# Token tiles staggered at stage ends, outputs by halves, own buffers for the last down piece, the gate through DRAM, four adaptive-norm chunks first

## The chip, the cores and the metric

One core of a Trainium2 chip. The time is the device time of one execution in microseconds; of a kernel before, the median of its runs is given. The kernel's two token tiles have 128 tokens each, all arithmetic is on 32-bit data.

## The reference, cut to what matters

Two blocks of two layers each run one after the other on x (256 tokens, 1024 channels). A layer has three stages, each of this form:

```
mod   = silu(c) @ ada_w[l] + ada_b[l]            # 9 x 1024 values: shift, scale, gate for 3 stages
n     = rmsnorm(x, g[j]) * (1 + scale[j]) + shift[j]
x     = x + factor * gate[j] * stage(n)          # first block: 1 + gate; factor 0.5 for an ffn, 1 for a mixer
ffn   : (silu(n @ w_gate) * (n @ w_up)) @ w_out  # 2816 hidden channels
mixer : layer 0 gated linear recurrence (hgrn2), 1 differential attention,
        2 and 3 sparse attention plus a gated mlp; each ends in an output projection 1024 x 1024
```

After layer 3 a last rmsnorm with its own gain. A stage is called (l,j) here, l from 0 to 3, j = 0 and 2 for an ffn, 1 for a mixer.

## The kernel before, in words

**Products.** TensorE multiplies each 32-bit product as three products of reduced-precision float parts: high by high, high by low, low by high (times_three, L1367). So each piece of weights (128 x 2048 values, 1 MB, two DMAs) that lands in `raw` (ring of 3) is cut: ScalarE writes its high part to `wH` (cut, L456), VectorE subtracts it for the low part `wL` (cut, L782). A piece may be loaded once the low part of the piece 3 before is done (s_split), and its high part is written once TensorE has used the piece 3 before (s_eaten). Everything that loads is issued by SyncE, in one order written out by hand.

**Ffn.** The hidden channels go in 11 groups of 256. A group has two up pieces (channels 0 to 3 and 4 to 7 of the input) and one down piece: 33 pieces, numbered 0 to 32. Group c's up products go into PSUM `GU` (bank i for token tile i), ScalarE takes silu of the gate half (L515), VectorE multiplies (L883) into `sh`, TensorE transposes it into `TM` (L1421), ScalarE writes the high part `hH` (L524), VectorE the low part `hL` (L887), and TensorE adds the down products into `PY` (two banks per token tile). TensorE's order in turn c: up piece 0, transposes of group c-1, up piece 1, down of group c-1, with both token tiles in each. At the end stand transposes and the down piece of the last group alone.

**Boundary** (boundary, L847, on VectorE; norm, L477, on ScalarE; norm_and_first, L1393, on TensorE). x tile i gets the gated output of `PY` (L841 scale over 1024 columns, L845 add); ScalarE squares it and takes the root; VectorE makes a diagonal matrix of 1/rms (L861); TensorE multiplies x by it, which transposes and scales (turn_x, L1385, L1389); VectorE (channels 0 to 3, L868) and ScalarE (4 to 7, L495) apply scale and shift; ScalarE and VectorE write high and low parts `xH` (L490) and `xL` (L874), two channels at a time; TensorE starts the first two pieces of the stage, tile 0 channels 0 to 5, turn_x of tile 1, then the rest. The pieces that are cut meanwhile: the next stage's piece 0 before the last hidden high part in ScalarE's queue, piece 1 ahead of the outputs, piece 2 at the end.

**Gate.** The gate is a column per 128 channels in `mod`. VectorE spreads it (L833), TensorE multiplies by the identity (gate_broadcast, L1378), ScalarE copies it to `gB`, where each partition has all 1024 values (L511).

**Adaptive norm.** The 18 chunks of 512 values of mod per layer are computed by VectorE, four products over 1024 values a chunk (L793), from 2 MB each. 8 chunks of layer 0 are done at the start through a ring of 5 in `M`, the other chunks one per group in the loops of the ffns: 10 in (l,0), 8 of the next layer in (l,2). Small constants of the mixers are loaded in (0,0) (late_constants, L379).

**Mixers** end in four projection pieces (project, L1494), each over both token tiles.

Of the kernel before, what the change touches and what calls it, by code (L numbers as in the profile page):

```python
# [116 lines left out]
def build(nc, T, out, upto=99):  # L117

    with ExitStack() as ctx:
# [20 lines left out]
        xL = sb("xL", [P, ND, S], F32R)  # L140
        hH = sb("hH", [P, 2, S], F32R)
# [11 lines left out]
        vb = sb("vb", [P, 5 * P])  # L153
# [12 lines left out]
        acc = sb("acc", [P, 4])  # L166
        modf = M[:, 0:2 * D].rearrange("p (t d s) -> p t d s", t=NT, d=ND)
# [50 lines left out]
        sg_ = [ada[:, n, :].rearrange("p (t n) -> p t n", t=NT) for n in range(2)]  # L218
        pec = sb("pec", [P, 2])
# [32 lines left out]
        s_x = sem("s_x")  # L252
        s_ss = sem("s_ss")
# [11 lines left out]
        s_gp = sem("s_gp")  # L265
# [50 lines left out]
        ADA_FIRST, ADA_REST = 8, 10  # L316
# [6 lines left out]
        def ada_turns(l, j):  # L323

            if j == 0:
                return l, ADA_FIRST, ADA_REST
            return (l + 1, 0, ADA_FIRST) if l + 1 < 4 else (l, 0, 0)

# [5 lines left out]
        def _(sp):  # L334
# [18 lines left out]
            def load_mixer(w, pieces):  # L353

                at = 0
                for k0, lo, width in pieces:
                    load(w[:, at:at + 4 * width], 4 * width)
                    at += 4 * width

            def load_start(c, q):  # L360
# [5 lines left out]
                sp.dma_start(start_[slot], T["ada_t"][0, 2 * c + q]).then_inc(s_start[slot], 16)  # L366
# [5 lines left out]
            def load_ada(l, c, q):  # L372
                v = T["ada_t"][l].rearrange("(c q) p n -> q p c n", q=2)
# [5 lines left out]
            def late_constants():  # L379
# [3 lines left out]
                for at, n, name in ((0, P, "a_onorm"), (P, P, "b_qk_g"), (2 * P, P, "b_subln"),  # L383
                                    (3 * P, 2 * P, "b_lam")):
                    sp.dma_start(vb[:, at:at + n], T[name].rearrange(
# [3 lines left out]
            def ffn(l, j):  # L389
                load_up(l, j, 0, 0)  # L390
                load_up(l, j, 0, 1)
                if (l, j) == (0, 0):
                    late_constants()
                if (l, j) == (1, 2):
                    sp.wait_ge(s_adafree, ADA_RING + 2 * (2 * ADA_REST + ADA_FIRST))
                    load_cond(1)
                la, c0, turns = ada_turns(l, j)

                def loop(first, count, with_ada):
                    with sp.Fori(0, count) as i:  # L400
# [4 lines left out]
                        if with_ada:  # L405
                            load_ada(la, c0 + i, 0)
                        load_up(l, j, first + i, 1)
                        if with_ada:
                            load_ada(la, c0 + i, 1)
# [1462 lines left out]
```

## Time and profile before

| | |
|---|---|
| median of 3 runs | 2488.42 us (2483.75 to 2490.06) |
| profiled execution | 2491.22 us, its span 2489.6 us |
| TensorE busy | 2273.3 us, 91% |
| VectorE busy | 1654.5 us, 66% |
| ScalarE busy | 1097.5 us, 44% |
| HBM read | 529.19 MB, 213 GB/s over the span |
| chain that ended last | TensorE 81%, VectorE 9%, ScalarE 5% |

Times are from the span's start. Busy time is a sum over the whole span; what a change at a boundary does is read from the timeline there. On TensorE's rows, the idle time in brackets counts from the end of the instruction before, which is modelled and overlaps the next one, so a product of 512 columns shows 0.39 us and follows the one before after 0.23. SPq rows are the issue of DMAs by SyncE, with the waits between merged issues inside. The ends of the 8 ffns are at about 259, 675, 871, 1226, 1423, 1854, 2050 and 2478, those of the 4 mixers at 477, 1027, 1657 and 2280.

### The profile page before, as it was taken

To read this page: it belongs to the slowest core of one execution; us is meant where nothing else is said; L and a number is where in the kernel's file an instruction comes from. 1 tells how busy PE (TensorE), PEld (TensorE's weight loads), DVE (VectorE), ACT (ScalarE), POOL (GpSimd) and SP (SyncE) were. 2 spreads that over 40 slices of the span, in tenths; PEclk is the share of its full clock that TensorE was granted. 3 is DMA by queue.
4 is the path that set the end of the run, shared out by engine and by line. 5 is a ranking of instruction groups with operands and counts; after the bars stand their busy time and mean duration, and the time that the engine had idled before them with its cause. 6 is when DMAs were issued, how large, how long until landed. Compare 5 with 4: busy or idle time off the path is not lost.

```text
span 2489.6 us, 30572 instructions
## 1 busy us (share of the span) xinstructions
PE 2273.3 (91%) x11004; PEld 1900.7 (76%) x11004; DVE 1654.5 (66%) x2245; ACT 1097.5 (44%) x1225; POOL 0.2 (0%) x4
## 2 busy tenths in 40 slices
PE   0999995899999997899999998999999999899998
PEld 0788884688788875788788787778878888777886
DVE  7677576677577776587577754468767776446444
ACT  1444543343444355434443444544344445464433
POOL 0000000000000000000000000000000000000000
PEclk9999997899999997999999997899999999799999
DMA  9687430388578731387588732348857883223553
GB/s 382 265 319 279 161 136 0 136 310 311 204 265 312 273 143 70 129 335 281 193 311 308 284 128 85 102 162 316 298 203 274 320 310 128 85 102 126 179 202 110
DMA packets 126426, 531.30 MB, mean 213 GB/s; under 512 B 14736, under 2 KB 15504, under 8 KB 107280
## 3 DMA queue, kind: packets, MB, share of 16 engines
q1 hardware_dynamic: 126352, 530.30, 58.8%
q8 instruction: 48, 0.79, 0.1%
q14 instruction: 26, 0.21, 0.0%
HBM read 529.19 MB, written 1.05 MB: 213 GB/s over the span
## 4 chain that ended last, share of the span: by engine, by line
PE 81%; DVE 9%; ACT 5%; issue 2%; DMA 2%; SPq 1%; DVEq 0%; ACTq 0%
PE GU L1371 14%; PE GU L1375 14%; PE GU L1373 14%; PE PY L1371 9%; PE PY L1373 9%; PE PY L1375 9%; DVE wL L786 2%; ACT wH L461 2%; PE PY L1389 2%; PE TM L1421 1%; DMA M<-in_ada_t 1%; PE GU L1758 1%; PE PY L1668 1%; DVE M L793 1%; DVE x L845 1%
## 5 line engine op out<-in xcount | busy, mean ns | idle before, releaser
L786 DVE TENSOR_TENSOR wL<-raw,wH 128x2048 fp32r<-128x2048 f32 x352 | 794.6, 2279 | 280.9 <-ACT wH L461 279.3
L461 ACT ACTIVATE wH<-raw 128x2048 fp32r<-128x2048 f32 x352 | 659.6, 1899 | 203.4 <-PE PY L1375 102.4
L1371 PE MATMUL GU<-wH,xH 128*128 128x512 f32 (+1 forms) x1600 | 635.2, 397 | 31.6 <-DVE xL L874 13.2
L1375 PE MATMUL GU<-wH,xL 128*128 128x512 f32 (+1 forms) x1600 | 623.8, 390 | 0.0
L1373 PE MATMUL GU<-wL,xH 128*128 128x512 f32 (+1 forms) x1600 | 623.3, 390 | 0.0
L1371 PEld LDWEIGHTS GU<-wH,xH 128*128 128x128 f32 x1600 | 302.8, 189 | 97.1 <-issue 32.6
L524 ACT ACTIVATE hH<-TM 128x512 fp32r<-128x512 f32 x88 | 52.7, 598 | 691.5 <-PE TM L1421 691.5
L1375 PEld LDWEIGHTS GU<-wH,xL 128*128 128x128 f32 x1600 | 302.3, 189 | 63.7
L1373 PEld LDWEIGHTS GU<-wL,xH 128*128 128x128 f32 x1600 | 303.0, 189 | 58.5
L793 DVE CUSTOM_DVE_ANT_0 ada<-ada,cond 128x1024 f32<-128x1024 f32 x256 | 298.0, 1220 | 0.0
L887 DVE TENSOR_TENSOR hL<-TM,hH 128x512 fp32r<-128x512 f32 x88 | 60.9, 691 | 253.8 <-ACT hH L524 253.7
L1371 PE MATMUL PY<-wH,hH 128*128 128x512 f32 x704 | 218.0, 391 | 12.5 <-DVE hL L887 12.4
L1373 PE MATMUL PY<-wL,hH 128*128 128x512 f32 x704 | 217.6, 390 | 0.0
L1375 PE MATMUL PY<-wH,hL 128*128 128x512 f32 x704 | 217.3, 390 | 0.0
L1371 PE MATMUL PY<-wH,xH 128*128 128x512 f32 x432 | 177.2, 410 | 8.2 <-DVE wL L786 6.8
L1373 PE MATMUL PY<-wL,xH 128*128 128x512 f32 x432 | 173.6, 402 | 0.0
L1375 PE MATMUL PY<-wH,xL 128*128 128x512 f32 x432 | 172.5, 399 | 0.0
L1371 PEld LDWEIGHTS PY<-wH,hH 128*128 128x128 f32 x704 | 131.7, 188 | 41.5 <-issue 10.3
L1375 PEld LDWEIGHTS PY<-wH,hL 128*128 128x128 f32 x704 | 132.7, 188 | 27.8
L1373 PEld LDWEIGHTS PY<-wL,hH 128*128 128x128 f32 x704 | 132.5, 188 | 27.7
L1371 PEld LDWEIGHTS PY<-wH,xH 128*128 128x128 f32 x432 | 84.8, 196 | 27.0 <-issue 5.5
L515 ACT ACTIVATE sh<-GU 128x512 f32<-128x512 f32 x88 | 52.7, 599 | 118.3 <-PE GU L1375 118.3
(275 smaller groups left out, 2013.9 us busy)
## 6 DMA issues: line engine op xcount, KB each, us to landing
raw<-in_up_w SPq DMA_DIRECT2D x352, 512.0 KB, 6.2
ada<-in_ada_t SPq DMA_DIRECT2D x128, 1024.0 KB, 8.1
raw<-in_down_w SPq DMA_DIRECT2D x176, 512.0 KB, 4.8
raw<-in_c_w SPq DMA_DIRECT2D x96, 512.0 KB, 4.3
raw<-in_a_w SPq DMA_DIRECT2D x40, 512.0 KB, 4.2
M<-in_ada_t SPq DMA_DIRECT2D x16, 1024.0 KB, 10.5
raw<-in_b_w SPq DMA_DIRECT2D x32, 512.0 KB, 4.3
M<-in_cmp_w SPq DMA_DIRECT2D x4, 1024.0 KB, 9.2
```

Of the source, the lines that this page charges most:

```text
L461: act.activation(wH[:, slot, 0:words], raw[:, slot, 0:words], ACT.Copy).then_inc(s_high, 1)
L515: act.activation(sh[:, 0, :, :], GU[:, :, 0:CF], ACT.Silu).then_inc(s_silu, 1)
L524: act.activation(hH[:, :, :].rearrange("p f s -> p (f s)"), TM[:, 0, :], ACT.Copy).then_inc(s_hh, 1)
L786: dve.tensor_tensor(wL[:, slot, 0:words], raw[:, slot, 0:words], wH[:, slot, 0:words], ALU.subtract).then_inc(s_split, 1)
L793: ins = dve.tensor_tensor_reduce(w, w, cond[:, :], 1.0, 0.0, ALU.mult, ALU.add, acc[:, 2 * q + b:2 * q + b + 1])
L845: dve.tensor_tensor(x[:, i, :], x[:, i, :], xn[:, i, :], ALU.add).then_inc(s_x, 1)
L887: dve.tensor_tensor(hL[:, :, :].rearrange("p f s -> p (f s)"), TM[:, 0, :], hH[:, :, :].rearrange("p f s -> p (f s)"), ALU.subtract).then_ ...
L1371: pe.matmul(outs[i], aH, wh[i], start=first, stop=False)
L1373: pe.matmul(outs[i], aH, wl[i], start=False, stop=False)
L1375: ins = pe.matmul(outs[i], aL, wh[i], start=False, stop=last)
L1389: ins = pe.matmul(PT[:, i, d, :], x[:, i, d * P:(d + 1) * P], diag[:, i, :], start=True, stop=True)
L1421: ins = pe.transpose(TM[:, 0, f * S + i * P:f * S + (i + 1) * P], sh[:, 1, i, f * P:(f + 1) * P], ident)
```

## The change

Start: 4 chunks instead of 8 at the start, x loaded after the fourth half; squares and roots of x between them. The chunks of the first block's layer 0 that follow: 10 in (0,0), one inside hgrn's second half after `q_` is gated, one after its last two low parts, 10 in (0,2). late_constants is issued after the last chunk's loop in (0,0).

Stage ends: in the last group of an ffn each step is done by token tile. The last down piece has its own `lastH`, `lastL`, tile 1's hidden parts their own `hHt`, `hLt`. Outputs are scaled and added by halves of 512 columns. The next stage's cuts may start a piece earlier. Mixers' last two pieces run tile 0 of both, then tile 1 of both. The last norm and the output DMA go by tile.

Gate: gcol is written to a DRAM tensor (`gates`, one row per stage, 1024 elements, not contiguous on the side of the core) and read back broadcast over 128 partitions, both by SyncE. The spread, the 8 products and the copy are gone.

The diff, cut; engine names are put ahead of hunks:

```diff
# SyncE
+            def gate_out():
+                n = t.next("gate")
+                sp.wait_ge(s_gcol, n)
+                sp.dma_start(T["gates"][n - 1].rearrange("(d p) -> p d", p=P), gcol[:, :],
+                             allow_slow_non_contiguous=True).then_inc(s_gd, 16)
+            def gate_in():
+                n = t.next("gate", 0)
+                sp.wait_ge(s_gd, 16 * n)
+                if n > 1:
+                    sp.wait_ge(s_x, NT * (n - 1))
+                sp.dma_start(gB[:, :], T["gates"][n - 1:n].broadcast_to([P, D])).then_inc(s_gb, 16)
-            def load_mixer(w, pieces):
+            def load_mixer(w, pieces, l):
...
+                    if l == 0 and n == 16:
+                        load_ada(MIXER_CHUNKS[0], 0)
+                        load_ada(MIXER_CHUNKS[0], 1)
+                    if n == 6:
+                        gate_out()
+                    if n == 10:
+                        gate_in()
...
                 if turns:
                     loop(1, turns, 1)
+                if (l, j) == (0, 0):
+                    late_constants()
                 if turns < NF - 1:
                     loop(1 + turns, NF - 1 - turns, 0)
+                gate_out()
                 load_down(l, j, NF - 1)
+                gate_in()
# ScalarE
+            def cut(words=PIECE, early=0):
+                slot, to = t.next("piece") % RING, t.next("weights") % RING
+                act.wait_ge(s_raw[slot], t.next(s_raw[slot], 32))
+                act.wait_ge(s_eaten, t.next(s_eaten) - early)
+                act.activation(wH[:, to, 0:words], raw[:, slot, 0:words], ACT.Copy).then_inc(s_high, 1)
+            def squares(i, first=False):
...
-                    root(i, (l, j) == PHASES[0])
-                    if i == 0:
-                        cut()
+                    if before:
+                        squares(i)
+                        root(i)
+                    if before and i == 0:
+                        cut(early=before == "ffn")
...
-                act.wait_ge(s_gp, t.next(s_gp))
-                act.activation(gB[:, :], TMf, ACT.Copy).then_inc(s_gb, 1)
+                cut(early=before == "ffn")
...
+                loop(NF - 2)
+                cut()
+                cut()
+                cut_last()
+                hidden_high()
                 if (l, j) != PHASES[-1]:
-                    cut()
-                hidden_high()
-                t.next("done")
+                    cut(early=1)
+                silu_tile(0)
+                high_tile(0)
+                silu_tile(1)
+                root_table()
+                high_tile(1)
# VectorE
+            def outputs_0(before):
+                dve.wait_ge(s_gb, t.next(s_gb, 16))
+                for h in range(2):
+                    dve.wait_ge(s_y, t.next(s_y))
+                    output(0, h)
+                if before == "ffn":
+                    low_tile(1)
...
                 columns(l, j)
-                cut()
-                if pieces:
-                    dve.wait_ge(s_gb, t.next(s_gb))
-                    dve.wait_ge(s_y, t.next(s_y))
-                    gated_output(0)
-                    add_output(0)
+                if before:
+                    outputs_0(before)
+                    root(0)
+                    scaled_identity(0)
+                    outputs_1(before, pieces)
...
-                        if pieces and i == 0 and b == 1:
-                            add_output(1)
+                        if before and i == 0 and b == 1:
+                            cut()
                 cut()
...
+                cut()
+                if turns == NF - 1:
+                    chunk(c0)
+                cut()
+                hidden_low()
+                cut_last()
+                hidden_tile(0)
                 if (l, j) != PHASES[-1]:
                     cut()
-                hidden_low()
+                low_tile(0)
+                hidden_tile(1)
# VectorE, hgrn
+                    if grp == 1:
+                        chunk(MIXER_CHUNKS[0])
...
                 cut()
                 cut()
+                chunk(MIXER_CHUNKS[1])
# TensorE
-                gate_broadcast()
                 turn_x(0)
                 slots = [t.next("piece") % RING for _ in range(2)]
-                pe.wait_ge(s_split, t.next(s_split, 2))
...
+                        if i == 0 and d % 4 == 0:
+                            pe.wait_ge(s_split, t.next(s_split))
...
+                        if by_tile and i == 0 and d == ND - 1:
+                            ins.then_inc(s_up, 1)
...
-                turn(True)
-                loop(NF - 2)
-                pe.wait_ge(s_h, t.next(s_h))
-                turn_hidden()
-                down(False, True)
+                pe.wait_ge(s_h, t.next(s_h))
+                token_tile(GU[:, 0, :], 0, slot, 0)
+                pe.wait_ge(s_h, t.next(s_h))
+                token_tile(GU[:, 1, :], 0, slot, 1).then_inc(s_eaten, 1)
...
+                loop(NF - 3)
+                pe.wait_ge(s_h, t.next(s_h))
+                up(0)
+                turn_hidden()
...
+                token_tile(GU[:, 0, :], 1, ups, 0).then_inc(s_up, 1)
...
+                down_tile(0, downs, False)
+                pe.wait_ge(s_h, t.next(s_h))
+                turn_tile(0)
+                token_tile(GU[:, 1, :], 1, ups, 1).then_inc(s_eaten, 1)
...
+                down_last(0)
+                pe.wait_ge(s_h, t.next(s_h))
+                turn_tile(1)
+                down_tile(1, downs, False).then_inc(s_eaten, 1)
+                pe.wait_ge(s_hl, t.next(s_hl))
+                down_last(1)
...
+            def project_last(q):
+                slots = [t.next("piece") % RING for _ in range(2)]
+                for i in range(NT):
+                    for h in range(2):
+                        if i == 0:
+                            pe.wait_ge(s_split, t.next(s_split))
+                        token_tile(PY[:, 2 * i + 1, :] if q is None else PY[:, 2 * i + h, :], h if q is None else q,
+                                   slots[h], i).then_inc(s_eaten if i else s_y, 1)
```

## Rows read from the trace of the kernel before

**Rows 1.** The page, part 1: busy time, share and instructions of each engine.
```profile
PE 2273.3 (91%) x11004; PEld 1900.7 (76%) x11004; DVE 1654.5 (66%) x2245; ACT 1097.5 (44%) x1225; POOL 0.2 (0%) x4
```

**Rows 2.** Waits of TensorE over the span: total us, times, longest.
```profile
PE PY L1371 <- DVE hL L887: 12.4, 8, 1.9
...
PE GU L1371 <- issue: 11.6, 8, 1.5
PE PY L1389 <- DVE M L861: 10.8, 12, 2.1
```

**Rows 3.** Timeline of the start: start us, us, instruction, idle before and releaser.
```profile
9.11 1.22 DVE L793 CUSTOM_DVE_ANT_0 M<-M,cond 128x1024 f32<-128x1024 f32 x1 [8.24 <-DMA M<-in_ada_t]
...
10.00:15.00 5.00, 0.00 (x0) 0.00 (x0) 4.93 (x10) 0.00 (x0) 0.00 (x0) 1.00 1.01 424
...
51.58 1.91 ACT L461 ACTIVATE wH<-raw 128x2048 fp32r<-128x2048 f32 x1 [44.88 <-DMA raw<-in_up_w]
...
67.09 0.77 PE L1371 MATMUL GU<-wH,xH 128*128 128x512 f32 x1 [3.92 <-DVE xL L874]
```

**Rows 4.** Timeline of the boundary from (0,2) to (1,0).
```profile
669.74 0.70 PE L1371 MATMUL PY<-wH,hH 128*128 128x512 f32 x2 [1.50 <-DVE hL L887]
...
672.98 1.22 DVE L841 TENSOR_TENSOR xn<-PY,gB 128x1024 f32<-128x1024 f32 x1
...
675.30 1.95 PE L1381 MATMUL TM<-cst,sh 128*128 128x128 f32 x16
...
677.70 2.05 PE L1389 MATMUL PY<-M,x 128*128 128x128 f32 x16 [0.45 <-DVE M L861]
...
680.81 0.47 PE L1371 MATMUL GU<-wH,xH 128*128 128x512 f32 x1 [1.06 <-DVE xL L874]
...
681.52 1.22 DVE L845 TENSOR_TENSOR x<-x,xn 128x1024 f32<-128x1024 f32 x1
...
695.26 0.47 PE L1371 MATMUL GU<-wH,xH 128*128 128x512 f32 x1 [1.46 <-issue]
```

**Rows 5.** Timeline of two boundaries after mixers, (0,1) and (1,1).
```profile
462.23 6.70 DVE L786 TENSOR_TENSOR wL<-raw,wH 128x2048 fp32r<-128x2048 f32 x3 [0.57 <-ACT wH L461]
...
484.46 0.77 PE L1371 MATMUL GU<-wH,xH 128*128 128x512 f32 x1 [0.24 <-DVE xL L874]
...
1027.08 1.95 PE L1381 MATMUL TM<-cst,sh 128*128 128x128 f32 x16
...
1031.12 3.46 PE L1389 MATMUL PY<-M,x 128*128 128x128 f32 x16 [2.10 <-DVE M L861]
...
1034.83 0.52 PE L1371 MATMUL GU<-wH,xH 128*128 128x512 f32 x1 [0.25 <-DVE xL L874]
```

**Rows 6.** Timelines of the start, (2,0) and (3,0); then issues by tile, KB, us to landing.
```profile
41.45 0.43 SPq L380 DMA_DIRECT2D cst<-in_table  x1
...
47.46 1.04 SPq L385 DMA_DIRECT2D vb<-in_b_lam  x1
...
1411.60 1.92 ACT L461 ACTIVATE wH<-raw 128x2048 fp32r<-128x2048 f32 x1 [2.11 <-DMA raw<-in_c_w]
...
2020.11 2.86 SPq L343 DMA_DIRECT2D raw<-in_down_w  x4
...
2031.38 0.60 PE L1421 MATMUL TM<-cst,sh 128*128 128x128 f32 x4
...
2039.66 1.92 ACT L461 ACTIVATE wH<-raw 128x2048 fp32r<-128x2048 f32 x1 [1.57 <-DMA raw<-in_c_w]
...
vec<-in_vec_cols SPq DMA_DIRECT2D x1, 240.0 KB, 4.4
...
posi<-in_positions SPq DMA_DIRECT2D x1, 1.0 KB, 14.8
```

**Rows 7.** Timeline of the end: first and last instruction of VectorE after the last product.
```profile
2478.92 1.23 DVE L841 TENSOR_TENSOR xn<-PY,gB 128x1024 f32<-128x1024 f32 x1 [0.17 <-PE PY L1375]
...
2483.75 1.29 DVE L1359 SCALAR_TENSOR_TENSOR x<-x,rstd,M 128x1024 f32<-128x1024 f32 x1
```

More of the change, by code:

```diff
@@ L576, in hgrn @@
             def hgrn():
-                norm(0, 1)
+                norm(0, 1, "ffn")
                 cut()
@@ L676, in nsa @@
             def nsa(l):
-                norm(l, 1)
+                norm(l, 1, "ffn")
                 cut()
@@ L767, in _ @@
                     nsa(l)
+                before = "mixer" if j == 1 else "ffn"
             if len(PHASES) == 12:
                 for i in range(NT):
+                    squares(i)
                     root(i)
@@ L847, in boundary, with chunk, output @@
-            def boundary(l, j, pieces):
+                    dve.tensor_scalar(gcol[:, :], gate, factor, None, ALU.mult).then_inc(s_gcol, 1)
+            def chunk(c):
+                ada_products(0)
+                ada_products(1)
+                ada_store(c, s_adafree, t.next(s_adafree, 2))
+            def output(i, h):
+                half = slice(h * 512, (h + 1) * 512)
+                chained(dve.tensor_tensor(xn[:, i, half], PY[:, 2 * i + h, :], gB[:, half], ALU.mult))
+                dve.tensor_tensor(x[:, i, half], x[:, i, half], xn[:, i, half], ALU.add
+                                  ).then_inc(s_x if h else s_xs, 1)
@@ new lines, in outputs_0, with outputs_1 @@
+            def outputs_0(before):
[5 more added lines that the diff above has]
+                    low_tile(1)
+            def outputs_1(before, pieces):
+                if before == "ffn":
+                    dve.wait_ge(s_y, t.next(s_y))
+                    t.next("done", pieces - 1)
+                else:
+                    dve.wait_ge(s_eaten, t.next("done", pieces - 1))
+                output(1, 0)
+                dve.wait_ge(s_eaten, t.next("done"))
+                output(1, 1)
@@ L1330, in _ @@
                 start_products(1)
-                ada_store(0, c, s_startfree, 2 * c + 2)
-            pieces = 0
-            for n, (l, j) in enumerate(PHASES):
-                if n == 0 or PHASES[n - 1][1] == 1:
-                    cut()
-                boundary(l, j, pieces)
+                ada_store(c, s_startfree, 2 * c + 2)
+                if c > 1:
+                    root(c - 2)
+                    scaled_identity(c - 2)
+            before, pieces = None, 0
+            for l, j in PHASES:
+                if before is None:
+                    cut()
+                if before != "ffn":
+                    cut()
+                boundary(l, j, before, pieces)
+                if j == 1:
+                    gate_column(l, j)
                 if j != 1:
@@ L1344, in _ @@
                     nsa(l)
+                before = "mixer" if j == 1 else "ffn"
                 pieces = 3 * NF if j != 1 else PIECES[l] - (22 if l > 1 else 0)
-            dve.wait_ge(s_gb, t.next(s_gb))
-            dve.wait_ge(s_y, t.next(s_y))
-            gated_output(0)
-            add_output(0)
-            dve.wait_ge(s_eaten, t.next("done", pieces))
-            gated_output(1)
-            add_output(1)
+            outputs_0(before)
             if len(PHASES) == 12:
@@ L1423, in turn_hidden, with down_tile, down @@
                 ins.then_inc(s_ht, 1)
-            def down(first, last):
+            def down_tile(i, slot, first):
+                for f in range(2):
+                    a = slice(i * P, (i + 1) * P)
+                    halves = [slice(f * D + h * 512, f * D + (h + 1) * 512) for h in range(2)]
+                    ins = times_three([PY[:, 2 * i + h, :] for h in range(2)], hH[:, f, a], hL[:, f, a],
+                                      [wH[:, slot, b] for b in halves], [wL[:, slot, b] for b in halves],
+                                      first and f == 0, False)
+                return ins
+            def down(first):
                 slot = t.next("piece") % RING
```

338 lines of the change are left out of this document (201 added, 137 removed).

## The prediction, made before the result was known

> **What bounds the kernel now.** The page comes first: TensorE is busy for 2273.3 of 2489.6 us [rows 1], so only the 216 us in which it isn't busy, and work that can be made shorter, are to be had. The waits of TensorE, summed, come next [rows 2]: apart from the wait at the very start they are small and regular. It waits 12.4 us (8 times 1.5) for the low part of the last hidden piece, 11.6 us (8 times 1.46) as "issue" after the first up pieces, 10.8 us for the diagonal of the norm. Each lies at a stage boundary. The timeline of the first stage [rows 3], of a boundary after an ffn [rows 4] and after a mixer [rows 5] shows what happens there, and SyncE's timeline with ScalarE's waits [rows 6] what the transfers do. Last the end of the kernel [rows 7].
>
> The profiled execution took 2491.2 us (span 2489.6, 1.6 around it), 2.8 above the median of 2488.4. I make the sum against 2491.2 and take 2.8 off.
>
> **Start (four chunks first).** The first x product starts at 67.09 [rows 3]. The first piece of weights arrived at 51.58 because 17 MB stood ahead of it. Four chunks mean 4.2 MB less. At 9.11 about 1.9 MB have landed (first product [rows 3]); 7 chunk halves, x and piece 0 (9.4 MB) follow at 424 GB/s [rows 3]: 22.3 us, so piece 0 is there at 31.4. VectorE is no faster: half a chunk needs two products of 1.22 [rows 3], and each of the last four halves waits for its MB, so the eighth ends at about 31, and with both roots behind it at 33. ScalarE's cut of piece 0 stands behind the second root in its queue: to 34.8. The low parts, 2 x 2.2 us, end at 39.4; the scale columns and the step to the first product (677.70 to 680.81 less 1.2 for the transposes, which have long been done [rows 4]: 1.9) give 41.4. Gain 25.7, bounds 20 (everything serial behind the second piece) and 29 (bytes alone). The 4 chunks moved cost VectorE 4.9 us each: two in a loop turn of (0,2), where it has 3 us to spare in 16.8, one in hgrn's tail under the output projection, and chunk 15 before the boundary, below.
>
> **End of an ffn.** With the tiles staggered, other products (a piece of 24 takes 5.56 us, 669.74 to 675.30 [rows 4], so 12 products 2.7) stand between each transpose and the product that needs its low part. The 1.5 us before the last down piece [rows 4] goes at all 8 ends: 12.4 [rows 2]. Then tile 0's output: before, its scaling began 2.3 us before the end of the last down piece, and from there to the diagonal took 4.7 (672.98 to 677.70 [rows 4]). Now tile 0 is complete 5.4 us before the end (down_last(0), then turn, down_tile(1), down_last(1)), halves overlap, so the diagonal is ready about 2 us early. The 2.4 us from 675.30, in which the broadcast of 1.95 hides, to 677.70 goes. Tile 1's last half (2 x 0.62) is ahead of VectorE's first modulation and gives back 0.2. So 2.2 x 7 = 15.
>
> **End of a mixer.** The stretch from the last projection to the first up product is 7.75 us at 1027.08 [rows 5], 6.9 and 7.7 at two like it. Left is the 3.1 us that turn_x(0) takes to the product plus 0.3: gain 4.3, 3.5, 4.3, and 0.9 at two of them for products at the lower clock (the transposes take 3.46 instead of 2.05 [rows 4, 5]): 13. In hgrn VectorE stands in the way: three low parts (462.23, 6.70 us [rows 5]), now with chunk 15 (4.9) among them, so it is free for output 0 only at 474.3, the diagonal comes at 478.6, and both halves of tile 1 run to 481. First up product 483.0 instead of 484.46 [rows 5]: gain 1.5. Together 14.7.
>
> **New waits inside the boundary.** Piece 1 of a stage is now cut on VectorE between the low parts of channels 3 and 4. Before, an add of 1.22 us stood there (681.52 [rows 4]) and hurt nobody. A cut of 2.29 ends at 683.84, the low part 0.43 later; TensorE has used up channels 0 to 3 at 683.6. Loss 0.75 at 11 boundaries: 8.2. After the first up pieces 1.46 was lost 8 times [rows 2, 4]. Tile by tile, silu of tile 0 could start 5 us earlier, but ScalarE now has cut (1.9) and table load (1.28) ahead of it and VectorE a cut; I work out 0.7 left, nothing in (0,0). Gain 0.76 x 7 + 1.2 = 6.5. Net of both -1.7.
>
> **The gate through DRAM.** Removed: on VectorE the spread, on TensorE the broadcast, on ScalarE the copy, all of them already hidden. Added: per stage one write of 1024 single elements, a wait for it on SyncE, one broadcast read of 512 KB. SyncE has every load behind that wait. The trace has no such write. The nearest from below is the vector load of 240 KB, 4.4 us to landing; from above the positions, 256 single elements, 14.8 us, but behind a table of 1.3 MB [rows 6]. I take 7, nearer to the lower, since the queue is nearly empty there; both ends stay in the range's cases. In a mixer four pieces lie between write and read and cover it. At an ffn's end the write goes out behind the load of piece 31 (the down piece before the last), the read and everything of the next stage behind it. Look at (3,0): piece 31 is issued at 2020.11 [rows 6], the write 2021.0, landed 2028. Then come the read and, ahead of the next piece, the mixer's own 3.2 MB: with piece 33 that is 4.8 MB, 11.4 us, so it lands at 2041 (before: cut at 2039.66, with ScalarE already waiting for it [rows 6]). Before, only the last hidden piece stood behind that cut. Now it stands ahead of the silu of tile 0, whose product TensorE needs two half pieces after the transposes of 2031.38 [rows 6], plus 5.4 and 0.44: at 2037.3. Cut 1.9 and silu and product 0.9: 2043.8. Stall 6.5. At (2,0) landing was already 1411.60 [rows 6]; by the same steps 6.6. At (0,0) the late constants are new before the write: 41.45 to 48.5, 7.05 us of issue [rows 6], 1.6 MB. Piece 32 and with it the low part stall 3, piece 33 another 3: 6. At (1,0), (0,2), (1,2), (2,2) piece 33 lands 1 to 4 us before it is needed: 0. After two of the stalls the clock will fall, as behind the gap of 4 us in [rows 5]: 1.4 (3.46 for 2.05), 1.5 each with what follows. Loss 6.5 + 6.6 + 6 + 3 = 22.
>
> The Trainium skill speaks against this edit too ("DMA: Bandwidth & Descriptors", Rules for kernel authors): a last dimension that isn't contiguous becomes one descriptor per element. Its "Anatomy of one DMA" puts a fixed cost of about 2 us on each DMA, most of it the receipt, heaviest toward HBM; neither is shown by a row here. With 2 us in the place of 7, an estimate by that page, the three stalls would be 15 us smaller; with many descriptors the rule points the other way.
>
> **End of the kernel.** From the last product (2478.75) to the last scaling (2483.75 + 1.29 [rows 7]) was 6.3 us, with a scale and an add of 1.23 each over 1024 columns and a square of 1.06. With halves, and tile 0 long done, 4.6; the last DMA is half as long. Gain 2.
>
> **Sum.** 25.7 + 12.4 + 15 + 14.7 - 1.7 - 22 + 2 = 46. 2491.2 - 46 - 2.8 = 2442.
>
> **Rivals.**
> A, the stalls don't come: the write lands in 3 us or less and the piece behind it is in time. For it: before, ScalarE waited only 1.6 us for this piece at (3,0) [rows 6]. Against: bandwidth alone, without any round trip, puts it at 2039.7, too late for 2037.3. With 5 of the 22 left: 2442 - 17 = 2425.
> B, the write takes 12 us: 5 more at the three stalled ends, 4 at two, 1 at two more: 25, so 2467.
> C, slower than before: the same place, SyncE waiting for the write with the next stage's loads behind it. With a us more than 7 the loss is 3a + 2(a - 1) + 2(a - 4); it eats the 46 at a = 8, so from a write of 15 us. At 20 us it is 81: 2523. For it: 1024 element writes are more pieces than any row here has, and they stand behind loads in flight. Against: the positions took their 14.8 us only behind 1.3 MB [rows 6].
> D, the stagger brings nothing: VectorE, with low parts, four output halves and a cut in one queue, has the diagonal late again. For it: hgrn's end is such a case. Against: at the end of [rows 4] I count 2 us of slack. Without the 15 and half of the 12.4: 2463.
>
> **How the numbers follow.** Forecast 0.5, A 0.2, B 0.12, C 0.06, D 0.12. Likeliest 2442. The range takes in A, B and D, and below A the start's better bound: 2420 to 2469; C is left out, with the tails of A and B. A difference below 0.3% (7.5 us) can't be told from none. Faster by more than that: all but C and the edge of B, 0.93; within 0.02; slower 0.05.
>
> **What would show it.** First up product near 41 instead of 67.09. The waits of the last down piece for the low part and of turn_x for the diagonal gone except in hgrn's. New waits of TensorE for the low part of piece 1 (0.75, 11 times) and, at the ends of (0,0), (2,0), (3,0), for the tile's hidden product, with ScalarE's cut waiting for a transfer. SyncE's wait for the write gives its time; well off 7 us moves the sum by 3 to 7 times the difference. The prediction is wrong if those three ends show no gap, or if ends without extra transfers show one.

## The result, and the profile after

The changed kernel takes 2511.8 us (median of 5, 2501.4 to 2521.1) against 2488.1 (median of 5) for the kernel before: ratio 1.0092, interval 1.007 to 1.0113. It is slower by 0.9%; 2442 was forecast. Its profiled execution took 2514.3 us, span 2512.5.

The page of the changed kernel: busy time by engine, DMA packets, the chain by engine and by line.

```profile
PE 2274.6 (91%) x10812; PEld 1888.1 (75%) x10812; DVE 1655.6 (66%) x2305; ACT 1095.3 (44%) x1289; POOL 0.2 (0%) x4
...
DMA packets 140656, 537.72 MB, mean 214 GB/s; under 512 B 27424, under 2 KB 28192, under 8 KB 121504
...
PE 73%; DVE 11%; DMA 7%; ACT 6%; issue 2%; SPq 1%; ACTq 0%; DVEq 0%
PE GU L1530 12%; PE GU L1534 11%; PE GU L1532 11%; PE PY L1530 9%; PE PY L1532 9%; PE PY L1534 9%; DVE wL L875 4%; DMA gates<-gcol 3%; ACT wH L504 3%; PE TM L1574 1%; DMA raw<-in_c_w 1%; DMA raw<-in_up_w 1%; PE PY L1777 1%; DVE ada L888 1%; PE PY L1874 1%
```

TensorE issues 192 products fewer than in [rows 1] and is busy as long: where products fell away, others ran at the lower clock. DMA stands for 7% of the chain, and 3% is the gate's write by name.

TensorE's waits (total us, times, longest), which answer to [rows 2]:

```profile
PE PY L1530 <- DVE hL L1010: 38.4, 8, 14.3
PE GU L1530 <- DVE xL L997: 31.6, 23, 9.6
PE TM L1610 <- DVE sh L1016: 28.2, 7, 9.9
```

then SyncE's wait for the write, and the two gate transfers with their KB and median us from issue to landing:

```profile
SPq L377 <- DMA gates<-gcol: 82.6, 8, 13.2
```

```profile
gB<-gates SPq DMA_DIRECT2D x12, 512.0 KB, 5.8
gates<-gcol SPq DMA_DIRECT2D x12, 4.0 KB, 12.2
```

4 KB take 12.2 us where I had taken 7. The wait for the hidden low part, which was to vanish, is three times its 12.4 of before, and the silu product of a tile (sh) is waited for at nearly every ffn end, not at three. The start went as forecast (answers to the last of [rows 3]):

```profile
40.37 0.77 PE L1530 MATMUL GU<-wH,xH 128*128 128x512 f32 x1 [9.64 <-DVE xL L997]
```

The end of (0,2), one of the four ends that I had put at 0. The timeline, SyncE, ScalarE and TensorE (answers to [rows 4]):

```profile
631.52 0.38 SPq L368 DMA_DIRECT2D gates<-gcol  x1
632.51 0.82 SPq L354 DMA_DIRECT2D raw<-in_down_w  x2
644.37 0.33 SPq L377 DMA_DIRECT2D gB<-gates  x1
...
646.09 1.91 ACT L511 ACTIVATE lastH<-raw 128x2048 fp32r<-128x2048 f32 x1 [7.64 <-DMA raw<-in_down_w]
647.91 0.58 ACT L584 ACTIVATE hH<-TM 128x512 fp32r<-128x512 f32 x1
652.61 1.91 ACT L504 ACTIVATE wH<-raw 128x2048 fp32r<-128x2048 f32 x1 [4.12 <-DMA raw<-in_up_w]
...
641.72 0.60 PE L1574 MATMUL TM<-cst,sh 128*128 128x128 f32 x4
...
649.36 0.70 PE L1530 MATMUL PY<-wH,hH 128*128 128x512 f32 x2 [4.28 <-DVE hL L1010]
655.30 0.44 PE L1610 MATMUL TM<-cst,sh 128*128 128x128 f32 x2 [1.36 <-DVE sh L1016]
...
666.83 1.95 PE L1541 MATMUL PY<-M,x 128*128 128x128 f32 x16
```

The load of piece 32 goes out 1 us behind the write and is there 13.6 us after its issue (646.09; before, a down piece took 4.8). ScalarE stands at its cut from 638.5. The transposes of the hidden part are done at 642.3, and their high part can't start before 647.91, because it is queued behind that cut. After the stall the staggered end does what it was to do: turn_x (TensorE's transposes of x tile 0, which open the next stage) starts at 666.83 with no wait at all, where it had waited for the diagonal. The same stretch in windows (us; busy time of each engine, granted clock, DMA share, GB/s):

```profile
630.00:636.00 6.00, 6.00 (x28) 4.99 (x27) 5.67 (x6) 2.41 (x2) 0.00 (x0) 1.00 0.97 306
636.00:644.00 8.00, 8.00 (x38) 6.60 (x38) 6.81 (x10) 1.92 (x1) 0.00 (x0) 1.00 1.13 77
644.00:655.00 11.00, 5.65 (x17) 3.72 (x15) 3.07 (x3) 4.58 (x4) 0.00 (x0) 0.84 0.91 295
```

The middle row is the one to look at: from 636 to 644 the DMA engines are busy throughout (1.13; the packets' times are added up, so the share can pass 1) and move 77 GB/s. At (0,0), with the late constants still in the queues, it is worse. TensorE alone, with its clock:

```profile
210.00:220.00 10.00, 6.89 (x33) 1.00 0.90 62
220.00:228.00 8.00, 0.00 (x0) 0.52 0.71 114
228.00:238.00 10.00, 5.81 (x15) 0.53 0.91 331
```

After 14.3 us without work TensorE goes on at 231.2 at half speed (granted clock 0.50 from 228 to 236, its 1.2 GHz level); from 236 to 238 the clock is 0.66, from 238 on 1.00.

### The profile page after: what moved, and what is told of

It is laid out like the page before. It is cut to its first block, busy times and chain, and to the rows that moved or that the text cites. A ratio compares the mean times of both kernels' runs of the same rounds, so it can differ in the third digit from the quotient of the medians.

```text
span 2512.5 us, 30163 instructions
## 1 busy us (share of the span) xinstructions
PE 2274.6 (91%) x10812; PEld 1888.1 (75%) x10812; DVE 1655.6 (66%) x2305; ACT 1095.3 (44%) x1289; POOL 0.2 (0%) x4
## 4 chain that ended last, share of the span: by engine, by line
PE 73%; DVE 11%; DMA 7%; ACT 6%; issue 2%; SPq 1%; ACTq 0%; DVEq 0%
PE GU L1530 12%; PE GU L1534 11%; PE GU L1532 11%; PE PY L1530 9%; PE PY L1532 9%; PE PY L1534 9%; DVE wL L875 4%; DMA gates<-gcol 3%; ACT wH L504 3%; PE TM L1574 1%; DMA raw<-in_c_w 1%; DMA raw<-in_up_w 1%; PE PY L1777 1%; DVE ada L888 1%; PE PY L1874 1%
## 5 line engine op out<-in xcount | busy, mean ns | idle before, releaser
L875 DVE TENSOR_TENSOR wL<-raw,wH 128x2048 fp32r<-128x2048 f32 x344 | 777.0, 2279 | 284.5 <-ACT wH L504 283.7
L504 ACT ACTIVATE wH<-raw 128x2048 fp32r<-128x2048 f32 x344 | 645.1, 1900 | 237.2 <-PE PY L1534 94.8
L1530 PE MATMUL GU<-wH,xH 128*128 128x512 f32 (+1 forms) x1600 | 640.5, 400 | 40.6 <-DVE xL L997 31.6
L888 DVE CUSTOM_DVE_ANT_0 ada<-ada,cond 128x1024 f32<-128x1024 f32 x272 | 316.7, 1221 | 0.0
L1530 PE MATMUL PY<-wH,hH 128*128 128x512 f32 x640 | 203.3, 399 | 39.6 <-DVE hL L1010 38.4
L1534 PE MATMUL PY<-wH,hL 128*128 128x512 f32 x640 | 201.3, 396 | 0.0
L1532 PE MATMUL PY<-wL,hH 128*128 128x512 f32 x640 | 200.9, 396 | 0.0
L1530 PEld LDWEIGHTS PY<-wH,hH 128*128 128x128 f32 x640 | 120.5, 191 | 69.2 <-issue 41.6
L1534 PEld LDWEIGHTS PY<-wH,hL 128*128 128x128 f32 x640 | 122.6, 192 | 26.2
L1532 PEld LDWEIGHTS PY<-wL,hH 128*128 128x128 f32 x640 | 122.5, 191 | 26.2
L1534 PEld LDWEIGHTS PY<-wH,xL 128*128 128x128 f32 x432 | 84.2, 195 | 18.6
```

Of the source, the lines that this page charges most:

```text
L504: act.activation(wH[:, to, 0:words], raw[:, slot, 0:words], ACT.Copy).then_inc(s_high, 1)
L875: dve.tensor_tensor(wL[:, to, 0:words], raw[:, slot, 0:words], wH[:, to, 0:words], ALU.subtract).then_inc(s_split, 1)
L888: ins = dve.tensor_tensor_reduce(w, w, cond[:, :], 1.0, 0.0, ALU.mult, ALU.add, acc[:, 2 * q + b:2 * q + b + 1])
L1530: pe.matmul(outs[i], aH, wh[i], start=first, stop=False)
L1532: pe.matmul(outs[i], aH, wl[i], start=False, stop=False)
L1534: ins = pe.matmul(outs[i], aL, wh[i], start=False, stop=last)
```

## Where the time went, stage by stage

From one stage's first product to the next one's, in us of each profiled execution, and beside it two experiments told below: the changed kernel without the write, and the kernel before with the write added.

| stage | before | after | after, no write | before + write |
|---|---|---|---|---|
| to the first product | 67.1 | 40.4 | 40.6 | 66.7 |
| (0,0) | 198.2 | 212.2 | 201.1 | 198.3 |
| (0,1) mixer | 219.2 | 218.1 | 218.3 | 219.2 |
| (0,2) | 196.4 | 199.6 | 191.9 | 196.3 |
| (1,0) | 195.8 | 200.4 | 191.9 | 195.7 |
| (1,1) mixer | 158.3 | 157.9 | 157.2 | 158.8 |
| (1,2) | 196.7 | 200.6 | 192.9 | 196.7 |
| (2,0) | 197.6 | 211.3 | 202.3 | 204.6 |
| (2,1) mixer | 235.3 | 231.9 | 231.5 | 234.5 |
| (2,2) | 195.8 | 201.6 | 192.2 | 195.8 |
| (3,0) | 195.8 | 208.9 | 201.4 | 204.5 |
| (3,1) mixer | 232.0 | 231.3 | 227.6 | 232.9 |
| (3,2) and end | 201.7 | 198.5 | 195.7 | 201.4 |

"After" less "after, no write": 7.5 to 11.1 us at each of seven ffns, 2.8 at the last. In the mixers it is 0.7 at most, but for 3.7 at (3,1), which no run explains.

## The experiments

### Is it the write, and is it SyncE's wait for it?

**The write away.** The read of 512 KB stays, but reads a norm gain, so the gate's values are others. SyncE's wait goes with the write:

```diff
-                sp.dma_start(T["gates"][n - 1].rearrange("(d p) -> p d", p=P), gcol[:, :],
-                             allow_slow_non_contiguous=True).then_inc(s_gd, 16)
...
-                sp.wait_ge(s_gd, 16 * n)
...
-                sp.dma_start(gB[:, :], T["gates"][n - 1:n].broadcast_to([P, D])).then_inc(s_gb, 16)
+                sp.dma_start(gB[:, :], T["final_g_2"].unsqueeze(0).broadcast_to([P, D])).then_inc(s_gb, 16)
```

> The gate isn't written to DRAM and SyncE doesn't wait; the broadcast read stays in its place but reads the last norm's gain, so the gate values used are others. Theory W: hidden waits about 20, time about 2445, close to what the prediction had (2442). Theory O: waits above 50, time above 2490. The difference to the kernel with the write is the write's whole price, by W 55 to 70 us.

Measured 2447.8 us, ratio 0.9842 (0.9825 to 0.9858). The write and its wait cost 64 us, in the profiled spans 67.9. TensorE's waits, and the DMA engines in a stretch near the same end of (0,2) (compare 77 GB/s above):

```profile
PE TM L1607 <- DVE sh L1013: 14.8, 2, 7.6
...
PE PY L1527 <- DVE hL L1007: 4.6, 1, 4.6
```

```profile
618.00:626.00 8.00, 8.00 (x37) 6.61 (x36) 7.67 (x6) 3.66 (x3) 0.00 (x0) 1.00 0.89 325
```

What is left is at (2,0), (3,0) and (0,0), the three ends that the prediction names, though no write is there any more.

**The write stays, the wait goes.** As above, but only the wait and the source of the read are changed; VectorE waits, a stage later, before it overwrites gcol.

> The write stays in its place, but the read is the same as in the run without a write (last norm's gain) and doesn't wait for it. This parts the two ways of the write: theory Wq (it is ahead of piece 32 in the DMA rings): the waits for the low part before down products, 38.4 us, stay above 30, and the waits for the tile's hidden product, 28.2, fall below 15: about 2485. Theory Ws (SyncE's wait behind it holds the next stage's loads): the first fall below 15, the second too: about 2450.

2507.5 us, 1.0082 (1.005 to 1.0115): 4 us of the 64, which is within the spread of these runs (2498.3 to 2515.4). TensorE waits 43.9 us for the hidden low part and 15.5 for the silu product, much as the first theory had it, but its time, 2485, is missed by 22 us. So SyncE's wait is not where most of the price is.

### Single elements, or a write as such?

```diff
-                sp.dma_start(T["gates"][n - 1].rearrange("(d p) -> p d", p=P), gcol[:, :],
-                             allow_slow_non_contiguous=True).then_inc(s_gd, 16)
+                sp.dma_start(T["gates"][n - 1].rearrange("(p d) -> p d", p=P), gcol[:, :]).then_inc(s_gd, 16)
```

> The write goes in the same place but as 128 pieces of 32 bytes (one row of the column tensor per partition), so the gate's values arrive permuted. Theory P (the price is per piece): the write lands in about 3 us, the time is about 2448, as without a write. Theory L (the price is a fixed latency of a write to DRAM behind loads in flight): still 9 us or more, and the time stays above 2490.

2450.6 us, 0.9856 (0.9839 to 0.9872), with the same place, bytes and wait; the gate's values arrive in another order. The issues of this kernel:

```profile
gates<-gcol SPq DMA_DIRECT2D x12, 4.0 KB, 4.3
```

128 pieces of 32 B land in 4.3 us, 1024 of 4 B in 12.2. So the price is in how the 4 KB are cut, not in a write to DRAM as such. The number of pieces and their size change together here; no run parts the two.

### Another queue

The write of the 8 ffns from ScalarE, ahead of its cut of piece 30:

> The changed kernel, the ffns' gate writes issued by ScalarE's queue at the same point (ahead of its cut of piece 30) instead of SyncE's; SyncE still waits for them before the read. Theory Q (the write holds piece 32 because both are in one queue's order): the waits for the hidden low part, 38.4 us, fall below 12, SyncE's wait stays near 10 us each; time about 2465. Theory E (the single elements keep the 16 engines themselves busy, whichever queue they are in): the waits stay above 30, time about 2500.

2512.6 us, 1.0096 (1.0079 to 1.0113), waits 43.2 (low part) and 25.9 (silu product). Issued from another engine, at 629.2 in (0,2) in place of 631.5, it stalls the same loads by as much. So the order within SyncE's queue is not the cause.

### Another place at the stage's end

**ScalarE's hidden high part ahead of its cut of piece 32**, with the wait and without:

```diff
-                cut_last()
                 hidden_high()
+                cut_last()
```

> The changed kernel with ScalarE's high part of the last hidden piece but one moved ahead of its cut of piece 32 (the last down piece). Theory E (the single elements of the gate's write hold piece 32 back, and the stall of TensorE comes because the hidden high part stands behind that cut): the last down product is needed 5.4 us later than the hidden part, so the waits for the hidden low part go at all ends but (0,0), where some 10 us of 14.3 are left, now before the last down product. But piece 33, whose time SyncE's wait for the write sets, comes no earlier, so the waits for the silu product grow by what went before them at the same end: (2,0) to 14, (3,0) to 12.8, others to 3 to 5. Sum of both 50 to 58 instead of 66.7, time 2496 to 2504. Rival F (piece 33 isn't bound by SyncE's wait): the sum falls to 35, time 2483. Rival G (order on ScalarE means nothing): unchanged, 2511.

> The run with ScalarE's hidden high part ahead of its cut of piece 32, now also without SyncE's wait for the gate's write (the gate is read from a norm gain instead, so its values differ; the write stays). Theory of two causes (write ahead of piece 32, and SyncE's wait ahead of piece 33): with both taken away the waits of TensorE at the ends are those of the run without any write plus what piece 32 lacks at (0,0): 15 + 8 = 20 to 30 us, time 2462 to 2475. Rival K (the elements alone hold piece 33 back too, whoever waits): waits 50 and more, 2490 to 2507.

2507.3 (1.0096, 1.0075 to 1.0116) and 2503.4 (1.0057, 1.0036 to 1.0078). TensorE's waits of the two:

```profile
PE TM L1610 <- DVE sh L1016: 71.6, 8, 16.8
```

```profile
PE TM L1611 <- DVE sh L1017: 71.4, 8, 16.4
```

The wait for the hidden low part is all but gone (1.8 and 0.3 us) and turns up whole at the next place (38.4 + 28.2 = 66.6 in the changed kernel), whether SyncE waits or not. The first run missed: a sum of 50 to 58 us and 2496 to 2504 were expected. The second refutes the theory of two causes, which had 20 to 30 us and 2462 to 2475; its rival K holds.

**The write behind the load of piece 32**, with the wait and without:

```diff
-                gate_out()
                 load_down(l, j, NF - 1)
+                gate_out()
                 gate_in()
```

> The changed kernel with the gate's write issued behind the load of piece 32 instead of ahead of it, SyncE still waiting for it before the read of the gate. Theory E with SyncE's wait: piece 32 lands in time, waits for the hidden low part at most 5 us in all (at (0,0)); piece 33 is issued one write time behind as before and lands no earlier, and TensorE now reaches it without the earlier stall, so the waits for the silu product are 45 to 62 us instead of 28, time 2495 to 2508. Rival H (only piece 32 matters, as the run without SyncE's wait but the same time seemed to say): 2450.

> The run with the gate's write behind the load of piece 32, now also without SyncE's wait for it (gate values from a norm gain). Here the elements stand directly ahead of piece 33, which before had 1 to 4 us to spare at four ends and none at (0,0), (2,0), (3,0). Theory (elements hold whatever comes behind them for some 8 us, whoever waits): the waits for the silu product are 30 to 50 us, time 2475 to 2495, between the run without a write (2448) and that with the wait (2519). Rival (only SyncE's wait makes piece 33 late): 2450.

2518.7 (1.0125, 1.0109 to 1.014) and 2506.3 (1.0061, 1.004 to 1.0081); waits for the silu product 59.0 and 43.5, for the hidden low part 15.0 and 18.0. Both times lie above what was expected (2495 to 2508 and 2475 to 2495), and the waits for the silu product inside it (45 to 62 and 30 to 50). The 15.0 us for the hidden low part were a miss as well: at most 5 had been expected, since piece 32 is now ahead of the write. At the end of (1,2) it was issued at 1191.8 to 1194.7, with the write directly behind it, and SyncE issues nothing else till 1207.5. ScalarE's cut of it, and the DMA engines just before (the last two numbers are their share and GB/s):

```profile
1206.87 1.91 ACT L511 ACTIVATE lastH<-raw 128x2048 fp32r<-128x2048 f32 x1 [7.08 <-DMA raw<-in_down_w]
```

```profile
1202.00:1207.00 5.00, 0.13 (x1) 1.00 0.00 0
```

Without a write the same cut waits 2.1 us. So the write can also hold a load that is ahead of it, and in these 5 us the profile shows no DMA engine at work. TensorE waits for the hidden low part at five ends, at one of which, (0,0), it does so without a write too; at the other three piece 32 is in time.

What the runs show is one write that makes both pieces late that the end of an ffn still needs, 32 and 33, in either order and from either queue. How it holds them is not shown: at (0,2) of the changed kernel the engines are busy at 77 GB/s, here they are idle. SyncE's wait is worth 4, 4 and 12 us in the three pairs by the medians, 3, 10 and 16 by the ratios to the kernel before measured beside each; the first two are at the edge of what these runs tell apart.

### The same write in the kernel before

```diff
+                gate_write()
                 load_down(l, j, NF - 1)
```

In the mixers it goes out ahead of the seventh piece, as in the changed kernel; nobody reads it and SyncE doesn't wait.

> The kernel before with the gate's write of 1024 single elements added at the places that it has in the changed kernel, and nothing else of the change (nobody reads it, SyncE doesn't wait for it). Theory: what the write costs hangs on how late its neighbours may be. At the end of (0,2) the load of piece 32 has 14.5 us from its issue until ScalarE must cut it in the old order (the cut is needed at 665.2, issue 650.7) against 9.2 us in the new one, where the hidden high part stands behind that cut; behind a write it lands 13.6 us after its issue. So in the old order nearly nothing is lost: 2489 to 2500. Rival (the write costs its 4 to 14 us at each of 8 ends in any order, as the run with the write but without SyncE's wait lost 60): 2530 to 2550.

2507.0 us, 1.0087 (1.0071 to 1.0102), so 20 us (15.8 in the spans), above the 0 to 11 expected and far below the rival. The stage table says where: 7.1 us at (2,0), 8.7 at (3,0), nothing at the other ffns. At the others the old order leaves piece 32 enough time: at (0,2) of this run it is issued at 646.7 and cut at 660.0, ScalarE waits 1.0 us for it, and TensorE's wait for the low part is the 1.50 of before. (The 14.5 us of the expectation count from 650.7; the kernel before issues the last two down pieces of that stage from 645.0 to 647.9.) At (2,0) ScalarE's cut of the mixer's first piece, with the own 3.2 MB and the write ahead of it, is what the last hidden part stands behind:

```profile
1418.86 1.91 ACT L472 ACTIVATE wH<-raw 128x2048 fp32r<-128x2048 f32 x1 [7.99 <-DMA raw<-in_c_w]
...
1423.84 1.19 PE L1384 MATMUL PY<-wH,hH 128*128 128x512 f32 x2 [8.93 <-DVE hL L900]
```

The same write costs 16 to 20 us in the old order and 58 to 60 in the new one (the run without SyncE's wait less the run without the write, spans and medians), 64 to 68 with the wait. The stagger brought the dates of pieces 32 and 33 forward and used up the slack that would have hidden it. At (0,0) this comparison isn't clean: only in the new kernel do the late constants stand directly ahead of the write.

### The write in the middle of the stage

Write after the fourth group of the ffn, read after the seventh, each in front of the next group's loads:

```diff
-                gate_out()
                 load_down(l, j, NF - 1)
-                gate_in()
...
+                    if n == 5:
+                        gate_out()
+                    if n == 8:
+                        gate_in()
```

> The gate's write goes out after the fourth group of each ffn and its read after the seventh, instead of around the last down piece; everything else as in the changed kernel, the late constants too. Theory W (the write of 1024 single elements takes 10 to 18 us and stands ahead of piece 32 and of SyncE's next loads): the waits of TensorE for the hidden parts at the ffn ends, 66.7 us, fall to about 25 (the late constants at (0,0), the mixers' own 3.2 MB at (2,0) and (3,0)), and the time to about 2450. Theory O (the new order of ScalarE's queue, the last piece's cut ahead of the hidden high part and the next stage's cut ahead of the tiles' silu, stalls by itself): the waits stay above 50, the time above 2490. Rival M: the write in the middle delays a piece there as much: waits move into the loops, the time stays about 2505.

2447.7 us, 0.9835 (0.9816 to 0.9854), the time of the kernel without a write. The write still takes 12.9 us, and in this profile nobody waits for it: TensorE's waits for low parts of weights are 9.3 us, as in the run without a write. Nothing of the computation is left out here, so this is the cure. It isn't free everywhere, as the next runs show. The waits left:

```profile
PE TM L1616 <- DVE sh L1022: 12.3, 2, 7.0
PE PY L1536 <- DVE hL L1016: 4.2, 1, 4.2
```

**The late constants there too.**

> As e1_mid, and the late constants too go out in the middle of (0,0), after its seventh group. If they and nothing else hold piece 32 there, the wait of 4.2 us for the hidden low part at the end of (0,0) goes and the time falls from 2447.7 to about 2442. If they were harmless, nothing changes; if they hold a piece in the middle, a wait of TensorE appears near 150 to 190 us.

2447.9, 0.9824 (0.9799 to 0.9848): a miss. The 4.2 us at (0,0) go, a wait of 1.5 for a silu product comes in its middle, and the stage takes 197.1 us in place of 200.7. In this profile the gain is lost again at (2,2), 196.4 in place of 192.4. There the gate's write goes out at 1685.8, the down piece behind the next loads is late, and TensorE waits for its low part:

```profile
1704.48 0.95 PE L1536 MATMUL PY<-wH,hH 128*128 128x512 f32 x2 [2.39 <-DVE wL L881]
```

**Then the next stage's first piece cut behind tile 0's hidden part**, on both engines:

```diff
-                if (l, j) != PHASES[-1]:
-                    cut(early=1)
                 silu_tile(0)
                 high_tile(0)
+                if (l, j) != PHASES[-1]:
+                    cut(early=1)
```

> As e5_late_mid, with ScalarE's cut of the next stage's first piece moved from ahead of tile 0's silu to behind its high part, and VectorE's cut with it. Theory: the 7.0 and 5.3 us at the ends of (2,0) and (3,0) come from that place in the queue, in front of which the mixer's own 3.2 MB lands late; they go, about 2429. Rival: the piece is late for tile 1's silu as well, half of it comes back there: 2436.

2437.5, 0.9789 (0.9772 to 0.9805): 10 us from the place of two cuts, about half of the 19 of the first theory, and close to the 2436 of its rival. The waits for the silu product fall from 13.1 to 4.3. In the spans (2,0) and (3,0) give 7.8 of the 10.3; (2,2) has its 4.1 back.

**Then the mixers' own 3.2 MB behind their first two pieces:**

> The fastest kernel so far (write in the middle of the stage, late constants there too, the cut of the next stage's first piece behind the hidden part of tile 0) with the own 3.2 MB of the mixers (2,1) and (3,1) issued behind their first two pieces instead of ahead of them. Theory: the two waits for the silu product that are left there (2.8 and 1.6 us) and up to 1 us at a lower clock go: 2432 to 2434 against 2437.5. Rival: later pieces of that mixer or the compression's weights come late in their turn, and it stays at 2437 or above.

2424.7, 0.976 (0.9747 to 0.9774), the fastest here: 13 us by the medians, 7 by the ratios, above the 3.5 to 5.5 expected. (2,0) took 200.8 us and takes 192.2, (3,0) 194.8 and takes 191.9. The waits for the silu product were 4.3. At (2,0) another 3.6 was a wait in the middle of the stage, for a down piece loaded behind the gate's write of 1251.2. This edit doesn't touch it, and yet it is absent from the new profile:

```profile
1271.10 0.77 PE L1536 MATMUL PY<-wH,hH 128*128 128x512 f32 x2 [3.58 <-DVE wL L881]
```

So a part of the 13 us isn't shown to belong to the edit.

### What four chunks first are worth by themselves

Eight chunks first again, none in hgrn, all else as in the run with the late constants in the middle:

> As e5_late_mid, but with 8 chunks at the start and none in hgrn, as in the kernel before. Prices the four chunks alone. Expected: first x product back from 40.4 to about 66, the end of (0,1) 1.5 us better: about 2466, 24 above e5_late_mid. If the four chunks' work comes back elsewhere in e5, the difference is smaller.

2467.5, 0.9927 (0.9902 to 0.9952): 20 us slower than with four, where 24 were expected. The first product is 20 us later than theirs, so the chunks cost nothing where they now stand:

```profile
60.76 0.76 PE L1526 MATMUL GU<-wH,xH 128*128 128x512 f32 x1 [9.66 <-DVE xL L996]
```

## Why the prediction was wrong

**The step that failed** is in "The gate through DRAM": "I take 7, nearer to the lower, since the queue is nearly empty there", and the sentence that says where it acts: "the write goes out behind the load of piece 31 (the down piece before the last), the read and everything of the next stage behind it". The size was wrong: 12.2 us. No row of the kernel before had so many pieces, and I stayed near the 240 KB load, by its bytes and the empty queue. The positions were no better guide: their 14.8 [rows 6] was the time of the table in front of them (15.0), and in the changed kernel they land after 7.0, behind the same table at 7.2. But size alone gives the 2467 of rival B, 45 us short. The place was wrong as well. I let the write cost only through what SyncE issues after it waited, that is piece 33, and treated the load of piece 32, issued 1 us behind the write, as not touched by it (at (0,0) it charged 3 us to the late constants). It was there 13.6 us after its issue. Hence "At (1,0), (0,2), (1,2), (2,2) piece 33 lands 1 to 4 us before it is needed: 0", where 7.7 to 9.4 us were lost each. Rival C had the sign, but not by its rule (from a write of 15 us): its mechanism, SyncE's wait, is worth 4 us (the run without it). The Trainium skill's rule, one descriptor per element where the last dimension isn't contiguous ("DMA: Bandwidth & Descriptors", Rules for kernel authors), which I had set beside the sum as a sentence of its own, pointed the right way. The traces agree: the changed kernel moves 12480 more packets under 512 B than the one without the write, 1040 for each of 12 writes of 1024 elements, and with 128 pieces of 32 B the write lands after 4.3 us.

**The clock.** 3 us were put down for it. Of the 67.9 between the spans with and without the write, TensorE's waits for the low part and the silu product explain 47.2 (66.6 less 19.4); TensorE's busy time grew by 21.9 (2274.6 for 2252.7) with the same 10812 products. After a stall the same products take longer, so a us of stall costs nearly one and a half here.

**What was luck.** Without the write the changed kernel runs in 2447.8, 5.8 from the forecast, and its span is 45.0 shorter than that of before; the sum of the prediction was 46. But that sum held 22 us of stalls that it put down to the write. For a write that costs next to nothing the prediction has rival A, with 5 of the 22 left: 2425. The kernel without a write is 23 us above that, and stalls for 19.4. So a second step failed too, that SyncE's wait of 7 us makes piece 33 late. At (3,0) without a write the DMA engines are busy from 1985 until the piece lands at 2001.6 (last two numbers: share and GB/s), so there it is the bytes ahead of it that take so long:

```profile
1985.00:2001.60 16.60, 4.44 (x3) 1.00 1.01 377
```

Two small slips stand in the sums beside this: 13 and 1.5 make 14.5 and not 14.7, and 2028 with 11.4 makes 2039.4, where the text has 2041 without a reason.

**What held.**

- Start: 25.7 forecast, 26.7 measured in the profile. With eight chunks first the first product came at 60.76: 20 of it are the chunks, and 6 the other edits of the start.
- An untroubled ffn end: 1.55 + 2.2 - 0.75 + 0.76 = 3.8 forecast. Gained without the write, by the stage table: 4.4, 3.9, 3.8, 3.6 at (0,2), (1,0), (1,2), (2,2). The stagger works; rival D is dead, and turn_x waits for no diagonal but in hgrn's end.
- Stalls without a write: the profile shows 7.6 and 7.2 at (2,0) and (3,0), 4.6 at (0,0); forecast 6.6, 6.5 and 6. The places are right and the sizes near, the cause is not (see above). Of the cause this much held at (2,0) and (3,0): ScalarE's cut of a piece that has the 3.2 MB ahead of it. In the fastest run, with both moved, no wait of that kind is left.
- Mixer ends: 14.7 less 4 times 0.75 makes 11.7; measured 0.9, 1.0, 3.8, 4.4, together 10.1. At (1,1) the boundary fell from 7.75 us [rows 5] to 3.4 as forecast, and inside the stage 3.4 came back: new waits of 1.2 us for a low part and 0.8 for xL, and TensorE's busy time 1.9 longer.
- The low part of piece 1: 0.75 forecast, 0.5 seen beside the 1.4 from turn_x to the first product.
- (3,2) and the end of the kernel: forecast 1.55 + 2 + 0.76 - 0.75 = 3.6, measured 6.0.

## What to carry to other kernels

The price of a small transfer isn't in its bytes: 12 writes of 4 KB cost 64 us here in 1024 pieces each, and 3 in 128 pieces each, which is within the spread. Most of it is paid by the loads beside it, even from another queue, and not by the one who waits for it; ask which loads are next and when they are due. Put such a transfer where its neighbours have time: in the middle of the stage the same write cost nothing in one profile and up to 4 us at a single stage in two others. And an edit that brings the last steps of a stage closer together uses up the slack of everything else that sits there, so two edits that are each harmless or cheap (the stagger, a write that costs 20 us in the old order) have to be priced together.

## What was not expected of the hardware

- A write of 1024 elements of 4 B to DRAM lands after 12.2 us (median of 12; 11.5 to 14.1 in eleven other kernels). With loads behind it the DMA engines show 8 us at a busy share of 1.13 and 77 GB/s, in place of 306 to 325. At (0,0), with the late constants in flight, SyncE went on 18.5 us behind it.
- With nothing behind it, a load of 1 MB issued ahead of it was there only after 12 us or more, and for the last 5 us the engines' share was 0.00.
- 128 pieces of 32 B with the same bytes land after 4.3 us.
- Issuing it on ScalarE's queue in place of SyncE's leaves the loads on SyncE's as late.
- In a stall of 14.3 us (216.9 to 231.2) TensorE's granted clock is 1.00 from 217 to 220, 0.52 from 220 to 228 and 0.50 to 236, with products running again from 231.2; from 238 it is 1.00.
